# Other planned durations for a kernel whose instruction order comes from a list scheduler: norm sums, convolution taps, pooling additions, scaled copies

## What is computed

```python
h = x
for layer in range(2):
    xn = rmsnorm(h, mix_norm_g[layer])
    if layer == 0:
        a, xb, gate_b, gate_c = split(xn @ ab_w_in)              # 4 x 512 columns
        a_out = pool_mixer(a, pool_w, pool_scale)                # 4 groups, trailing windows 2/4/8/16
        b_out = gate_b * short_conv(gate_c * xb, conv_w, conv_b) # 3 taps
        mix = concat([a_out, b_out]) @ ab_w_out
    else:
        ...                                                      # spatial gating, stick-breaking attention
    h = h + mix
    hn = rmsnorm(h, mlp_norm_g[layer])
    h = h + square(relu(hn @ mlp_w1[layer])) @ mlp_w2[layer]
return rmsnorm(h, final_norm_g)
```

## Time and profile before

| | |
|---|---|
| time, median of 3 runs | 2603.14 us (2600.72 to 2603.9) |
| profiled execution | 2602.82 us |
| its span on the slowest core (core 6) | 2601.3 us |
| spans of the 8 cores | 2588.6 to 2601.3 us |
| mean granted TensorE clock of the 8 cores | 0.991 to 0.994 |
| PE / DVE / ACT / POOL busy | 97% / 61% / 43% / 25% |

### The profile page before, as it was taken

How to read it: one execution, slowest core, us unless ns; L and a number is a source line. 1 busy time by engine, 2 the same in 40 slices (tenths; PEclk the granted TensorE clock), 3 DMA queues, 4 the chain that set the end, 5 groups by cost and what they waited for, 6 DMA issues and landing times.

```text
span 2601.3 us, 38509 instructions; the slowest of 8 cores (2588.6 to 2601.3 us)
## 1 busy us (share of the span) xinstructions
PE 2523.2 (97%) x12055; PEld 1108.3 (43%) x12055; DVE 1583.2 (61%) x2344; ACT 1117.3 (43%) x1749; POOL 658.0 (25%) x1088
## 2 busy tenths in 40 slices
PE   6899999999999999999999999999999999999996
PEld 2344444444444444444444444444444444444342
DVE  4761338567586565457577533677666777767554
ACT  3335223464335643174333444345543465345432
POOL 4531111212112253611245211212212122112121
PEclk9999999999999999999999999999999999999998
DMA  9777885745446897887572233433444335435544
GB/s 186 148 139 153 175 183 132 179 98 131 120 124 153 152 181 155 213 264 231 176 210 84 70 104 104 132 102 86 123 121 134 98 90 118 117 97 165 181 146 144
DMA packets 216686, 371.81 MB, mean 143 GB/s; under 512 B 90208, under 2 KB 98016, under 8 KB 216480
## 3 DMA queue, kind: packets, MB, share of 16 engines
q0 software_dynamic: 79664, 238.86, 38.3%
q1 hardware_dynamic: 136240, 129.36, 16.9%
q10 hardware_dynamic: 576, 1.05, 0.1%
HBM read 308.62 MB, written 95.42 MB: 155 GB/s over the span
## 4 chain that ended last, share of the span: by engine, by line
PE 91%; DVE 3%; DMA 3%; issue 2%; ACT 1%; SPq 0%; POOL 0%; DVEq 0%; ACTq 0%; POOLq 0%
PE ps L1400 62%; PE ps L1524 20%; PE ps L1616 6%; DMA h<-xT 2%; PE ps L2283 1%; PE ps L2240 1%; DVE xn L1416 1%; DMA ring<-wcm 1%; DVE Y L1416 1%; SPq L1721 0%; ACT ps L1409 0%; PE ps L2101 0%; DVE h L1413 0%; DVE xn L1413 0%; DVE mix L1413 0%
## 5 line engine op out<-in xcount | busy, mean ns | idle before, releaser
L1400 PE MATMUL ps<-xn,ring 128*128 128x512 bf16 x4960 | 1113.5, 381 | 9.0 <-DVE mix L1413 5.3
L1413 DVE TENSOR_TENSOR h<-ps,h 128x512 f32<-128x512 f32 x816 | 553.3, 688 | 526.2 <-PE ps L1400 295.3
L1400 PEld LDWEIGHTS ps<-xn,ring 128*128 128x128 bf16 x4960 | 473.9, 98 | 578.1 <-issue 20.8
L1409 ACT ACTIVATE ps<-ps 128x512 f32<-128x512 f32 x644 | 375.0, 583 | 703.2 <-PE ps L1400 324.7
L1338 POOL DMA_DIRECT2D ring<-wcm x269 | 143.9, 536 | 779.9 <-PE ps L1400 268.0
L1524 PE MATMUL ps<-hid,ring 128*128 128x512 bf16 x1408 | 327.6, 380 | 2.6 <-DMA ring<-wcm 2.2
L1409 ACT ACTIVATE hid<-ps 128x512 bf16<-128x512 f32 x496 | 294.4, 598 | 37.0 <-ACT ps L1409 1.9
L1338 POOL DMA_DIRECT2D ring<-wsc x308 | 165.9, 539 | 487.7 <-PE ps L1400 189.4
L1409 ACT ACTIVATE xn<-h 128x2048 bf16<-128x2048 f32 (+1 forms) x98 | 154.0, 1591 | 311.9 <-DVE h L1413 291.8
L1400 PE MATMUL ps<-hid,ring 128*128 128x512 bf16 x1280 | 281.0, 380 | 0.0
L1524 PE MATMUL ps<-TT,ring 128*128 128x512 bf16 x1056 | 255.4, 381 | 3.8 <-ACT ps L1409 3.1
(11 more groups left out here) (123 smaller groups left out, 1694.2 us busy)
## 6 DMA issues: line engine op xcount, KB each, us to landing
ring<-wsc POOLq DMA_DIRECT2D x308, 256.0 KB, 3.1
ring<-wblk POOLq DMA_DIRECT2D x188, 256.0 KB, 5.6
ring<-wcm POOLq DMA_DIRECT2D x93, 512.0 KB, 4.0
ring<-wcm POOLq DMA_DIRECT2D x118, 384.0 KB, 4.0
wsc<-ring SPq DMA_DIRECT2D x116, 256.0 KB, 4.2
wcm<-TT SPq DMA_DIRECT2D x64, 256.0 KB, 2.8
oT<-stg SPq DMA_DIRECT2D x56, 256.0 KB, 5.8
wcm<-ring SPq DMA_DIRECT2D x52, 256.0 KB, 4.1
```

The source lines that it names most:

```text
L1400: ins = pe.matmul(out, lhsT=l, rhs=r, start=(i == 0), stop=(i == n - 1), **({"skip_group_check": True} if skip else {}))
L1409: return self.S.op("act", lambda e: e.activation(out=out, in_=in_, func=func, **kw), rd=rd, wr=wr, dur=0.17 + n * 0.00083, aset=aset)
L1413: return self.S.op(eng, lambda e: e.tensor_tensor(out=out, in0=a, in1=b, op=op), rd=rd, wr=wr, dur=dur)
```

## The change

Nothing that is computed changes. Planned durations get other values, and a per-operation margin replaces the constant in one line. The core of the diff:

```diff
+RMARG = 0.6
+PMARG = 0.6
...
-                 "sig", "chan", "val", "val2", "vc", "waits", "succ", "npend", "ready", "aset", "boost", "tight")
+                 "sig", "chan", "val", "val2", "vc", "waits", "succ", "npend", "ready", "aset", "boost", "tight", "marg")
...
+        o.marg = MARGIN
...
-                    r = end if e == "pe" else (r if x.tight else r + MARGIN)
+                    r = end if e == "pe" else (r if x.tight else r + x.marg)
...
         def sums():
-            self.tt("dve", xn[:, t, 0:4, :], xn[:, t, 0:4, :], xn[:, t, 4:8, :], ALU.add, tx, tx[0:4], 1.22)
-            self.tt("dve", xn[:, t, 0:2, :], xn[:, t, 0:2, :], xn[:, t, 2:4, :], ALU.add, tx[0:4], tx[0:2], 0.69)
-            self.tt("dve", xn[:, t, 0, :], xn[:, t, 0, :], xn[:, t, 1, :], ALU.add, tx[0:2], tx[0:1], 0.43)
+            self.tt("dve", xn[:, t, 0:4, :], xn[:, t, 0:4, :], xn[:, t, 4:8, :], ALU.add, tx, tx[0:4], 1.29)
+            self.tt("dve", xn[:, t, 0:2, :], xn[:, t, 0:2, :], xn[:, t, 2:4, :], ALU.add, tx[0:4], tx[0:2], 0.74)
+            self.tt("dve", xn[:, t, 0, :], xn[:, t, 0, :], xn[:, t, 1, :], ALU.add, tx[0:2], tx[0:1], 0.52)
         def boosted(f, x):
             def g():
...
                 o.boost = RB
+                o.marg = RMARG
         def rstd1():
...
-            self.act(self.ms[m][:], self.bap(bi), AF.Ln, [self.t_bank[bi], self.t_cf], [self.t_ms[m]], 512, aset="ln",
+            self.act(self.ms[m][:], self.bap(bi), AF.Ln, [self.t_bank[bi], self.t_cf], [self.t_ms[m]], 620, aset="ln",
                      scale=1.0 / D, bias=self.cf[:, 60:61])
-            self.act(self.ms[m][:], self.ms[m][:], AF.Exp, [self.t_ms[m]], [self.t_ms[m]], 512, aset="ln", scale=-0.5)
+            self.act(self.ms[m][:], self.ms[m][:], AF.Exp, [self.t_ms[m]], [self.t_ms[m]], 555, aset="ln", scale=-0.5)
         def apply(c0, c1):
             def f():
...
                     self.mms(self.bap(bi), [(self.cb[:, 128 + g * 128:256 + g * 128], pb[:, c:c + 512])],
-                             [self.t_cb, self.t_pb], [self.t_bank[bi]], 0.25).boost = PB
-                    self.act(mx[:, t, g, :], self.bap(bi), AF.Copy, [self.t_bank[bi], self.t_cf], [tm[t][g]], 512,
+                             [self.t_cb, self.t_pb], [self.t_bank[bi]], 0.25).marg = PMARG
+                    self.act(mx[:, t, g, :], self.bap(bi), AF.Copy, [self.t_bank[bi], self.t_cf], [tm[t][g]], 620,
                              scale=cf[:, 40 + g:41 + g])
...
-                self.act(Y[:, 0:W], PR[:, 2:2 + W], AF.Identity, [self.t_PR, self.t_cf], [self.t_Y], W, scale=w2, bias=b)
+                self.act(Y[:, 0:W], PR[:, 2:2 + W], AF.Identity, [self.t_PR, self.t_cf], [self.t_Y], W * 1.26, scale=w2, bias=b)
-                         [self.t_Y], 0.15 + 1.15 * fw)
+                         [self.t_Y], 0.15 + 1.41 * fw)
-                         [self.t_Y], 0.15 + 1.15 * fw)
+                         [self.t_Y], 0.15 + 1.41 * fw)
...
-                            [td], 0.15 + 1.9 * fw)
+                            [td], 0.15 + 2.0 * fw)
...
-                S.op("pe", fz, rd=rk + [tm[t][4 + a]], wr=zt, dur=0.25, boost=ZB)
+                S.op("pe", fz, rd=rk + [tm[t][4 + a]], wr=zt, dur=0.28, boost=ZB)
```

## The result

The changed kernel is slower: 2612.88 us against 2603.26 us in the medians. The ratio is 1.0025, with a 95% interval of 1.0015 to 1.0036, so about 6.5 us. It lies on the side that I held least likely, and 2 us above my range.

A forecast was written before the change was run, and what follows sets the result against it. PE was taken as the bound, busy 2523.2 of 2601.3 us. Swapped pieces gain 3.8 us, half taken back, so -1.9 us against 2602.82 gives 2600.9; forecast 2601 us, range 2592 to 2611.

The forecast's parts named there:

- what I had called wrong altogether: Sign against the prediction: a large move of PE's idle time into the attention or MLP stages, outside the named stretches.
- The margins: RMARG and PMARG stay 0.6 as MARGIN is, and the removed boost was 0.0; claimed cost 0.
- The operation between the two taps: Layer-0 convolution: two `stg` on DVE between the taps, 3.50 us, claimed to stay whatever the due times.
- the worst wait on `mix`: Layer 0: PE waits 2.58 us after a slow first tap and two `stg`; the pattern was claimed to stay.
- the window 2560 to 2602: Last norm and stores: 23.6 us of PE idle time, where an order has little to choose.
- The small waits: PE's waits, nearly all in layer 0; on `mix`, `pb` and the sums together claimed to remain 12 to 22 us.
- I take half the gain back: Some 30 other layer-0 places get reordered without aim; takes 1.9 us from the 3.8 us gain, net -1.9 us.
- The other sum of the prediction: Layer-0 taps: by the DVE/GpSimd port lock no single duration describes a tap, so waits stay; 0 change, 2603 us.
- an order has little to choose: First 60 us (loading, first norm): 19.0 us of PE idle time, each step feeding the next.
- the 16.0 us behind ACT's squares: PE's waits behind ACT's squares, 16.0 us, taken as the kernel's start and end.
- The slower rival: Layer 0 and 2330 to 2560: weight loads land behind POOL additions, 6.1 us each; 2609 to 2615 us, chance 0.24.
- I costed that part at 0: Attention's score product, 0.25 to 0.28 us: moves PE's plan 3.8 us, due times move along, so cost 0.

The follow-up runs named there:

- before_earlyx: Kernel before the change, all durations kept, with sequence 1's first input loads planned readable 3.5 us earlier; ratio 1.0031.
- conv_padd: Kernel before the change with only the convolution's and the pooling additions' planned durations changed together; ratio 1.0016.
- after_latex: Changed kernel, all new durations kept, with sequence 1's first input loads planned to be readable 8.5 us later; ratio 1.0002.
- no_convpadd: Changed kernel with the convolution's and the pooling additions' planned durations back at their old values; ratio 0.9997.
- only_z: Kernel before the change with only the score product's planned duration changed, 0.25 to 0.28 us; mean span 2594.4 us against 2593.5 (cores 0 to 3, all executions).
- norm_latex: Kernel before the change with the norm's new durations and sequence 1's first input loads planned to land later; ratio 0.9982.

## Why the prediction was wrong

**Where it was right.** The counts and PE's busy time stayed (2523.1 against 2523.2). Not so the clock, which I had at 0.98 to 0.99 in layer 0: in 60 to 130 it is 0.93 on the slowest core. There is also a first sign of what I had called wrong altogether, 5.4 us idle in the attention stretch 860 to 1000 of that core, but only 1.3 us more than before as a mean. The margins did nothing that I had to explain. The operation between the two taps stayed, and so did the worst wait on `mix`; this is the stretch of the earlier trace rows after the change:

```profile
1344.37 1.27 DVE L1419 SCALAR_TENSOR_TENSOR Y<-PR,cfs,Y 128x1024 f32<-128x1024 f32 x1
1344.94 5.21 POOL L1416 TENSOR_TENSOR X<-X 128x1032 f32<-128x1032 f32 x2
1345.56 5.14 DVE L1419 SCALAR_TENSOR_TENSOR stg<-h,cfs,ms 128x512 f32<-128x512 f32 x2
...
1350.63 1.27 DVE L1419 SCALAR_TENSOR_TENSOR Y<-PR,cfs,Y 128x1024 f32<-128x1024 f32 x1
...
1353.31 5.30 PE L1403 MATMUL ps<-xn,ring 128*128 128x512 bf16 x16 [2.58 <-DVE mix L1416]
```

The wait is 2.58 us to the last digit. The tap that took 2.92 us now takes 1.27, but the two `stg` between the taps take 5.14 instead of 3.50: the collision with POOL moved by one instruction. Taps range from 1271 to 3185 ns, against 1272 to 2935.

One slip in its sums: the window 2560 to 2602 ends 0.7 us behind the span, so the end holds 22.9 us and not 23.6. Nothing hangs on it.

**Where it failed.** Three steps.

The term "I take half the gain back", which made the net -1.9 us. It priced reordering as PE pieces that swap places, with a gain of 3.8 us and half of it as loss. The small waits did move about as I had thought: on core 7 `mix`, `pb` and the sums together are 4.9 + 9.3 + 0 = 14.2 us against 7.2 + 3.7 + 5.5 = 16.4. As means over the cores, `mix` and the sums gave 6.8 us, more than the 3.8 I had, but `pb` alone took 6.0: not half of the gain went back, but nearly all. What the term left out altogether was ACT's list. One swap there cost 4.9 us of waiting as a mean, more than my whole gain. The other sum of the prediction, 2603 us with the waits where they are, fails at the same step.

The reading of the first 60 us and of the 16.0 us behind ACT's squares as a start in which "an order has little to choose". The load that lands at 65 us belongs to that start and reaches into the tightest stretch. ACT's idle time of 5.83 us before its square, harmless in the trace of before since nobody waited behind it, was the trap. I never looked at ACT's timeline there.

The slower rival. It had the right kind of mechanism, an instruction queued behind another on its engine, but the wrong queue: weight loads behind POOL additions. That its price (6.1 us) is near the measured loss (6.5) is luck. PE's waits on `ring` are 6.7 us after and 4.7 before as means over the cores, so this rival gave 2 us at most. The mechanism that it should have named was ACT's copies behind a square whose load is late.

**What is shown and what isn't.** Shown: squares ahead of the `PA` copies make PE wait 5 to 6 us, with no changed duration too, and that kernel is slower by as much as the whole change (before_earlyx); the convolution and the additions together produce that order (conv_padd); planning the load later removes the wait, and the loss goes, with all durations kept (after_latex). Neither of the two edits of the load separates the wait from everything else that they reorder. Not shown is that the wait is the whole loss: 3.3 of the 8.1 us of added idle time lie in its stretch. Not settled: why the additions alone cost 3.5 us without it; the 2.0 us of mean idle time added in 1340 to 1500, of which conv_padd shows 0.6 and the additions alone 2.0; and the waits on `AT`. They are 1.1 to 2.1 us as means in the four kernels with the new score duration (after, after_latex, no_convpadd, only_z) and 0.2 to 0.8 in eight of the ten others, but before_earlyx (1.2) and norm_latex (1.3) are as high without it. I costed that part at 0, and no time contradicts it; about 1 us may hide there.

## What to carry to other kernels

In a schedule made from planned times, a more exact duration is no improvement by itself: what counts is whether an instruction that waits for something uncertain is put ahead of one that others need. Look in the trace for long idle times of an in-order engine before an instruction that waits for a load, harmless ones too, and make the plan's time for that load fit first; here a landing planned 8.5 us later was worth the whole loss. And read more than one execution: the profile of one kernel here hid a loss of 3.5 us that its eight executions show. A mean duration is itself a product of the order: the smallest norm sum had a mean of 524 ns, was planned with 0.52, and has 417 ns in the new order.

## What was unexpected in the hardware

Mean durations moved with the order without any change of an instruction: the last norm sum from 524 to 417 ns, the first pooling addition from 2165 to 2011 ns (much the same on other cores, 524 to 525 against 417 to 419 and 2159 to 2190 against 2003 to 2011), which the earlier trace rows would explain by what the other engine does beside them; no run isolates that.

```profile
L1416 POOL TENSOR_TENSOR X<-PA 128x1038 f32<-128x1038 f32 x16 | 32.2, 2011 | 10.2 <-ACT PA L1412 9.8 <-PE ps L1403 0.2
...
L1416 DVE TENSOR_TENSOR xn<-xn 128x512 bf16<-128x512 bf16 x37 | 15.2, 417 | 0.7
```

The cores of one execution, with the same program and no exchange between them, differ more than the effect that was looked for: 2592.7 to 2610.9 us after the change, and the wait on `PA` alone 2.9 to 6.9 us. And in norm_latex a core showed a clock of 0.81 over 60 to 200 us with PE hardly waiting (0.9 and 0.4 us idle), so a clock between its two levels there had no waits of PE beside it (core 0):

```profile
60.00:130.00 70.00, 69.12 (x261) 0.81 0.64 132
130.00:200.00 70.00, 69.56 (x263) 0.81 0.67 124
```
